# Two-layer encoder trunk: the MLP's first product in seven block products instead of eight

## The reference

```python
def sq_relu_mlp(xn, w_up, w_down):
    return jnp.square(jax.nn.relu(xn @ w_up)) @ w_down

def reference(x, ...):
    h = x
    for l in range(DEPTH):
        hn = rms_norm(h, mix_norm_g[l])
        ...
        hn = rms_norm(h, mlp_norm_g[l])
        h = h + sq_relu_mlp(hn, mlp_w_up[l], mlp_w_down[l])
    return rms_norm(h, final_norm_g)
```

## Time and profile before

| | |
|---|---|
| median of 3 runs | 2364.94 us (2364.88 to 2365.31) |
| span of the profiled execution | 2362.9 us |
| TensorE busy | 2332.4 us, 14581 matmuls |
| VectorE, ScalarE, GpSimd busy | 1462.6, 1090.2, 249.8 us |
| read from HBM | 422.79 MB, 180 GB/s |
| mean granted TensorE clock | 0.998 |
| first relu of the two MLPs | 569.04 and 1656.99 us after the span's start |

### The profile page before, as it was taken

How to read it: one execution, slowest core, us unless ns; L and a number is a source line. 1 busy time by engine, 2 the same in 40 slices (tenths; PEclk the granted TensorE clock), 3 DMA queues, 4 the chain that set the end, 5 groups by cost and what they waited for, 6 DMA issues and landing times.

```text
span 2362.9 us, 38313 instructions
## 1 busy us (share of the span) xinstructions
PE 2332.4 (99%) x14581; PEld 2108.1 (89%) x14581; DVE 1462.6 (62%) x1686; ACT 1090.2 (46%) x1391; POOL 249.8 (11%) x367
## 2 busy tenths in 40 slices
PE   8999999999999999999999999999999999999997
PEld 6888888789899999999989999998998998998996
DVE  5777777755565565565566564656555556555655
ACT  5555554435444444444445334345444444444443
POOL 4445555500000000000000000000000000000000
PEclk9999999999999999999999999999999999999999
DMA  9555555455555555555555555555555555555553
GB/s 257 162 154 157 145 152 166 145 177 170 189 192 181 192 182 194 180 193 182 190 188 176 187 180 183 192 179 178 194 180 194 181 193 182 191 183 189 189 184 125
DMA packets 316175, 425.78 MB, mean 180 GB/s; under 512 B 10537, under 2 KB 141906, under 8 KB 315986
## 3 DMA queue, kind: packets, MB, share of 16 engines
q1 hardware_dynamic: 316066, 424.92, 56.4%
q10 hardware_dynamic: 48, 0.02, 0.0%
HBM read 422.79 MB, written 2.10 MB: 180 GB/s over the span
## 4 chain that ended last, share of the span: by engine, by line
PE 87%; POOL 6%; issue 4%; ACT 1%; DVE 1%; SPq 1%; DMA 0%; POOLq 0%; DVEq 0%; ACTq 0%
PE pair L353 14%; PE pair L355 14%; PE pair L357 14%; PE m L379 11%; PE m L377 11%; PE m L375 11%; PE pair L379 3%; PE pair L375 3%; PE pair L377 3%; POOL lk L577 1%; PE m L726 1%; POOL even L564 1%; POOL kin L577 1%; PE m L790 1%; POOL lk L589 1%
## 5 line engine op out<-in xcount | busy, mean ns | idle before, releaser
L337 DVE TENSOR_TENSOR w_lo<-raw,w_hi 128x1024 fp32r<-128x1024 f32 x800 | 988.8, 1242 | 855.5 <-ACT w_hi L326 854.5
L326 ACT ACTIVATE w_hi<-raw 128x1024 fp32r<-128x1024 f32 x800 | 846.2, 1059 | 1219.3 <-PE pair L357 633.6
L379 PE MATMUL m<-xT_hi,w_lo 128*128 128x256 f32 x2176 | 615.8, 283 | 0.0
L377 PE MATMUL m<-xT_lo,w_hi 128*128 128x256 f32 x2176 | 615.8, 283 | 0.0
L375 PE MATMUL m<-xT_hi,w_hi 128*128 128x256 f32 x2176 | 615.6, 283 | 0.0
L353 PE MATMUL pair<-w_hi,yT_hi 128*128 128x512 f32 x1280 | 499.8, 391 | 1.0 <-DVE h L1208 0.9
L355 PE MATMUL pair<-w_lo,yT_hi 128*128 128x512 f32 x1280 | 498.4, 389 | 0.0
L357 PE MATMUL pair<-w_hi,yT_lo 128*128 128x512 f32 x1280 | 498.1, 389 | 0.0
L375 PEld LDWEIGHTS m<-xT_hi,w_hi 128*128 128x128 f32 x2176 | 417.7, 192 | 1.2
L377 PEld LDWEIGHTS m<-xT_lo,w_hi 128*128 128x128 f32 x2176 | 417.7, 192 | 1.2
L379 PEld LDWEIGHTS m<-xT_hi,w_lo 128*128 128x128 f32 x2176 | 417.7, 192 | 0.0
(11 more groups left out here) (147 smaller groups left out, 1711.0 us busy)
## 6 DMA issues: line engine op xcount, KB each, us to landing
raw<-in_mlp_w_up SPq DMA_DIRECT2D x128, 1024.0 KB, 5.2
raw<-in_mlp_w_down SPq DMA_DIRECT2D x128, 1024.0 KB, 5.0
raw<-in_ab_w_in SPq DMA_DIRECT2D x256, 256.0 KB, 3.9
raw<-in_conv_w_in SPq DMA_DIRECT2D x48, 1024.0 KB, 5.2
raw<-in_ab_w_out SPq DMA_DIRECT2D x64, 256.0 KB, 4.1
raw<-in_conv_w_out SPq DMA_DIRECT2D x16, 1024.0 KB, 5.0
h<-in_x SPq DMA_DIRECT2D x4, 512.0 KB, 5.9
out_dram<-h SPq DMA_DIRECT2D x8, 256.0 KB, 2.4
```

The source lines that it names most:

```text
L326: nc.scalar.activation(w_hi[:, ring], raw[:, slot, 2 * k:2 * k + 2], ACT.Copy).then_inc(hi_ready, 1)
L337: nc.vector.tensor_tensor(w_lo[:, ring], raw[:, slot, 2 * k:2 * k + 2], w_hi[:, ring].bitcast(F32), ALU.subtract).then_inc(lo_ready, 1)
L377: nc.tensor.matmul(dst[:, c], w_hi[:, ring, q, cols], xT_lo[:, kt], start=False, stop=False)
L379: mm = nc.tensor.matmul(dst[:, c], w_lo[:, ring, q, cols], xT_hi[:, kt], start=False, stop=end and c % 2 == 1)
```

## The change

The first 1024 hidden columns of an MLP stay plain, as two blocks, but with the tokens in the partitions: the normalised x is stationary (128 tokens), 512 weight columns are moving. The other 7168 columns come in seven rounds of 1024. In a round X is seen as 2x2 blocks (128 tokens by 1024 features) and the weights as 2x2 blocks B11, B12, B21, B22 of 1024 by 512, and the 2x2 result is formed by Strassen's scheme in Winograd's form: seven products P1 to P7, each of 24 matmuls of 512 columns over two slots, where plain blocks need eight.

- The sums of x (`x_sums`) are made once per MLP from an unsplit copy (`x_pair`), then split.
- Four sums of weight blocks are made in place, in two halves of 128x2048: B11+B12, then B12+B22, B11+B22 and B11+B21, the last two into the same buffer. VectorE makes five of the eight halves (`block_sum`), GpSimd issues an accumulating DMA within SBUF for three, the second halves of P7, P6 and P4.
- The order of a round is P1 D0 P5 D1 P7 D2 P6 D3 P3 D4 P4 D5 P2 D6 D7, where D0 to D7 are the slots of the second product of the round before (`down`). Some products accumulate in one PSUM bank; ScalarE copies four partial results out (`copy`), VectorE adds five times (`combine`).
- The result has tokens in the partitions, so TensorE transposes each block (`turn`, four transposes) after relu and square.
- Buffers: `raw` has 8 MB, three pairs of it for blocks and four halves for the second product's weights, which are loaded by half slots of 512 KB; the mixer's tiles now share memory with them. xT is laid out by token halves.

The diff, cut to its core:

```diff
+ROUNDS = FF // 1024
+ROUND = ["P1", "D0", "P5", "D1", "P7", "D2", "P6", "D3", "P3", "D4", "P4", "D5", "P2", "D6", "D7"]
+ROUND_AT = {name: sum(2 if u[0] == "P" else 1 for u in ROUND[:k]) for k, name in enumerate(ROUND)}
+ROUND_SLOTS = 22
+PLAIN = 8
+TAIL_AT = PLAIN + (ROUNDS - 1) * ROUND_SLOTS
+MLP_SLOTS = TAIL_AT + 8
+BLOCK_OF = {"P1": "B11", "P5": "B11", "P7": "B12", "P6": "B11", "P3": "B22", "P4": "B11", "P2": "B21"}
+SUM_OF = {"P5": ("B11", "B12"), "P7": ("B12", "B22"), "P6": ("B11", "B22"), "P4": ("B11", "B21")}
+SUMS = ["P5", "P7", "P6", "P4"]
+SUMS_DVE = [("P5", 0), ("P5", 1), ("P7", 0), ("P6", 0), ("P4", 0)]
...
+        blocks = [raw[:, 4:6], raw[:, 0:2], raw[:, 2:4]]
+        raw_d = raw[:, 6:8].rearrange("p a (b c) n -> p (a b) c n", b=2)
...
+        FORM = {"P1": (xT_hi[:, 0, 0:8], xT_lo[:, 0, 0:8]),
+                "P2": (xT_hi[:, 0, 8:16], xT_lo[:, 0, 8:16]),
+                "P4": (xT_hi[:, 1, 8:16], xT_lo[:, 1, 8:16]),
+                "P3": (xT_hi[:, 1, 0:8], xT_lo[:, 1, 0:8]),
+                "P5": (s_hi[0], s_lo[0]), "P6": (s_hi[1], s_lo[1]), "P7": (s_hi[2], s_lo[2])}
...
+                def load_block(r, block, free):
+                    if r == ROUNDS:
+                        return
+                    kt, col = 8 * (block[1] == "2"), 1024 * r + 512 * (block[2] == "2")
+                    buf = buffer_of(r, block)
+                    for k in range(2):
+                        if free is not None:
+                            sp.wait_ge(lo_ready, 2 * (free + k) + 2)
+                        sp.dma_start(blocks[buf][:, k], up[:, kt + 4 * k:kt + 4 * k + 4, col:col + 512]
+                                     ).then_inc(landed_b[buf][k], 16)
+                def load_down(r, m):
+                    cb, half = m // 2, half_of(r, m)
+                    for k in range(2):
+                        n = d_at(layer, r, m, k)
+                        if r == 1 and m < 2:
+                            sp.wait_ge(s_low, 4 * layer + (4 if (m, k) == (1, 1) else 3))
+                        else:
+                            two = (r, m - 2) if m > 1 else (r - 1, m + 6)
+                            sp.wait_ge(lo_ready, 2 * slot_of(at, two[0], f"D{two[1]}") + k + 1)
+                        kt = 8 * (r - 1) + 4 * half + 2 * k
+                        sp.dma_start(raw_d[:, n % 4], down[:, kt:kt + 2, cb * 512:(cb + 1) * 512]
+                                     ).then_inc(landed_d[n % 4], 16)
...
+                load_plain(5)
+                load_plain(6)
+                load_plain(7)
+                load_block(1, "B12", at + 4)
+                load_block(1, "B22", at + 6)
+                load_down(1, 0)
+                load_down(1, 1)
+                for r in range(1, ROUNDS):
+                    load_down(r, 2)
+                    load_down(r, 3)
+                    load_block(r, "B21", slot_of(at, r, "P7"))
+                    load_down(r, 4)
+                    load_down(r, 5)
+                    load_block(r + 1, "B11", slot_of(at, r, "P3"))
+                    load_down(r, 6)
+                    load_block(r + 1, "B12", slot_of(at, r, "P4"))
+                    load_down(r, 7)
+                    load_block(r + 1, "B22", slot_of(at, r, "P2"))
+                    load_down(r + 1, 0)
+                    load_down(r + 1, 1)
...
+            def mlp(at, layer):
+                for r in range(1, ROUNDS):
+                    for name in ("P7", "P6", "P4"):
+                        to, other = SUM_OF[name]
+                        a, b = buffer_of(r, to), buffer_of(r, other)
+                        pool.wait_ge(landed_b[b][1], block_landed(layer, r, other))
+                        if name == "P7":
+                            pool.wait_ge(sums.sem, sums.at("P51", nth(layer, r)))
+                        else:
+                            last = {"P6": "P5", "P4": "P6"}[name]
+                            pool.wait_ge(lo_ready, 2 * (slot_of(at, r, last) + 1) + 2)
+                        pool.dma_start(blocks[a][:, 1], blocks[b][:, 1], accum_op=ALU.add
+                                       ).then_inc(added[name], 16)
...
+                def product(r, name):
+                    n = nth(layer, r)
+                    if name == "P1" and r > 1:
+                        pe.wait_ge(c_made.sem, c_made.at("C22", n - 1))
+                        pe.wait_ge(copied.sem, copied.at("C21", n - 1))
+                    if name == "P7" and r > 1:
...
+                    more = name in ("P6", "P3", "P4")
+                    hi, lo = FORM[name]
+                    at_slot = slot_of(at, r, name)
+                    for k in range(4):
+                        ring = (2 * at_slot + k) % HALVES
+                        pe.wait_ge(lo_ready, 2 * at_slot + k + 1)
+                        for q in range(2):
+                            kt = 2 * k + q
+                            nc.tensor.matmul(BANK[name], hi[:, kt], w_hi[:, ring, q],
+                                             start=kt == 0 and not more, stop=False,
+                                             skip_group_check=more)
+                            nc.tensor.matmul(BANK[name], hi[:, kt], w_lo[:, ring, q],
+                                             start=False, stop=False, skip_group_check=more)
+                            mm = nc.tensor.matmul(BANK[name], lo[:, kt], w_hi[:, ring, q],
+                                                  start=False, stop=kt == 7,
+                                                  skip_group_check=more)
+                        mm.then_inc(w_used, 1)
...
+                def turn(r, c):
+                    n = made(layer, r, c)
+                    pe.wait_ge(c_sq, n)
+                    if n > 1:
+                        pe.wait_ge(c_lo, n - 1)
+                    for q in range(4):
+                        ins = nc.tensor.transpose(M[3][:, q * P:(q + 1) * P],
+                                                  c_block(c)[:, q * P:(q + 1) * P], ident[:])
+                    ins.then_inc(c_T, 1)
...
+                for r in range(1, ROUNDS):
+                    for name in ROUND:
+                        if name[0] == "P":
+                            product(r, name)
                         else:
-                            down(p - 4, at + 4 + p, 8, i, i)
-                pe.wait_ge(pair_read[0], before)
...
+                            down(r, int(name[1]))
+                        if name == "P1":
+                            turn(r - 1, "C12" if r == 1 else "C11")
+                        if name == "D0" and r == 1:
+                            turn(0, "C22")
+                        if name in ("P3", "P4", "P2"):
+                            turn(r, {"P3": "C22", "P4": "C12", "P2": "C21"}[name])
+                turn(ROUNDS - 1, "C11")
...
+                            xT_hi[:, :, kt], of_tokens(M[b], q), ACT.Copy,
                             scale=gains[:, GAIN_OF[n] + kt:GAIN_OF[n] + kt + 1])
+                        if n % 2:
+                            ins = nc.scalar.activation(
+                                x_pair(kt), of_tokens(M[b], q), ACT.Copy,
+                                scale=gains[:, GAIN_OF[n] + kt:GAIN_OF[n] + kt + 1])
                     ins.then_inc(norm_hi[n], 1)
...
+                def square(r, c):
+                    n = made(layer, r, c)
+                    if r == 0:
+                        src, scale = pair[c[2] == "2"][:, int(c[1] == "2")], 1.0
+                        if n % 4 in (3, 0):
+                            eng.wait_ge(c_T, n - 2)
+                    else:
+                        eng.wait_ge(c_made.sem, c_made.at(c, nth(layer, r)))
+                        src, scale = c_block(c), -1.0 if c in ("C12", "C22") else 1.0
+                    nc.scalar.activation(c_block(c), src, ACT.Relu, scale=scale).then_inc(c_relu, 1)
+                    eng.wait_ge(c_relu, n)
+                    nc.scalar.activation(c_block(c), c_block(c), ACT.Square).then_inc(c_sq, 1)
...
+                for r in range(1, ROUNDS):
+                    for name in ROUND:
+                        slot = slot_of(at, r, name)
+                        if name == "D0":
+                            hidden_hi(r - 1, "C12" if r == 1 else "C11")
+                        if name == "P5" and r == 1:
+                            hidden_hi(0, "C22")
+                        if name in ("D4", "D5", "D6"):
+                            hidden_hi(r, {"D4": "C22", "D5": "C12", "D6": "C21"}[name])
+                        if name == "D4":
+                            copy(r, "C21")
+                        split(slot + 2)
+                        if name[0] == "P":
+                            split(slot + 3)
+                        if name in ("P1", "P5", "P6"):
+                            copy(r, {"P1": "P1", "P5": "C22", "P6": "C12"}[name])
+                        if name in ("D3", "D4", "D5", "D6"):
```

(54 more changed lines are left out.)

503 lines of the change are left out of this document (321 added, 182 removed).

## The result

The changed kernel takes 2352.06 us (median of 4 runs, 2350.45 to 2354.02) where the kernel before takes 2364.93 on the same chip: ratio 0.9945, 95% interval 0.9931 to 0.996. It is 12.9 us faster. The forecast was 61 us faster, and 2352 lies above 2348, the top of its range. The profiled execution has a span of 2350.0 us, 2.1 less than the median.

A forecast was written before the change was run, and what follows sets the result against it. The prediction took TensorE's instruction stream to bound the two MLPs: 2364.9 less 91.4 of TensorE work, plus 21 of lateness in the rounds and 9 at the MLP starts, gave 2303.5, stated as 2304, range 2275 to 2348 us.

The forecast's parts named there:

- Where it is late: Walk of three engines through a round and each MLP start: TensorE late 1.5 us a round (21 us), 9 at the starts.
- the paragraph on SP's queue: Second-product weight loads: D7's the tightest, landed near 69, wanted at 71, covered by 2 us; if not, 14 us.
- Spacings 0.120 and 0.2267 us: Start-to-start distances of 256- and 512-column matmuls on TensorE; the wider form saves 20.4 us per layer.
- Transposes 0.1 each: New TensorE transposes of the hidden block: 128 a layer at 0.1 us each, 12.8 us.
- VectorE 72.3 us a round: VectorE's splits, block sums, combinations and hidden low parts in a round, against 83.2 us of TensorE: 87% busy.
- A round of 84.8: Length of a round expected in the changed profile, about 84.8 us; TensorE's own work in it 83.2.
- P5 late by 0.4: In each round P5's first low part ends at 11.7 us, TensorE wants it at 11.3: late 0.4.
- P6 late by 1.1: In each round P6's low part comes at 34.4 us, wanted at 33.5: late 0.6, and 0.5 in its next entries.
- The accumulating DMA at 10 us: Each of three a round taken as twice a plain load, 10 us; P7's has 12 us free, so no cost.
- The third rival: Kernel slower because P7's accumulating DMA is the bound: at 20 us, 9.2 late a round and 2432 us; chance 12%.
- Second rival: VectorE binds in the product slots: 87.4 us a round, 4.2 above TensorE's 83.2, kernel at 2341 us; chance 16%.
- The norm block's extra activations: Eight more ScalarE activations a layer: 8.0 us in two slots, swallowed by four entries of lead; otherwise 3.6 a layer.

The follow-up runs named there:

- e1: Changed kernel with the unsplit copies of x in memory free at that time, so D0's loads wait less: 2341.54 us, ratio 0.99.
- e2: Changed kernel with only the hidden blocks' high and low parts moved earlier in ScalarE's and VectorE's queues at each MLP start: 2315.61 us, ratio 0.9793.
- w_wide: Kernel before, first product with x stationary and 512 weight columns moving, needed transposition left out: 2323.67 us, 41.3 us less, ratio 0.9828.
- v0: e4 without VectorE's five half sums and the waits for them, so part of the computation is missing: 2290.86 us, ratio 0.9687.
- d0: e4 without the three accumulating DMAs a round and ScalarE's waits for them, so three half sums are missing: 2306.18 us, ratio 0.975.
- g1: e4 with the high and low part of the fourth sum of x made later: 2301.76 us, ratio 0.9735, the fastest full version.
- f1: e4 with the second half of P5's block sum made after P5's first low parts: 2344.55 us, ratio 0.9913.
- e4: Changed kernel with the edits of e1 and e3 together, the fourth low part in D1's step: 2306.28 us, ratio 0.975.
- e3: Changed kernel with e2's edits, three sums of x split one slot earlier and the fourth high part after the squares: 2308.23 us, ratio 0.9758.

## Why the prediction was wrong

**The step that failed** is one sentence of "Where it is late": at the start of each MLP "4.5 us a layer, 9 in both". The stops are 20.9 and 20.5 us, and the lower clock behind them costs about 12 more. (The two terms of that sentence, 3.0 and 1.1, add to 4.1 and not 4.5; it changes nothing here.) Three things were left out:

1. I walked VectorE's work at the start only up to D0 and P5, and never asked what D0's buffer was used for until then. The diff has the answer in one line, `sp.wait_ge(s_low, ...)`: the load of D0 waits for VectorE. In the paragraph on SP's queue only D7 was walked, the tightest load of a running round; the first of the first round was the late one. e1 prices it at 10.5 us.
2. `turn` waits for a low part that stands in VectorE's order behind two splits or two sums. I counted it as 2.4 us of work in the round, and not as a wait of TensorE with work queued in front. e2 prices it at 36.4 us with its share of the clock, the high part on ScalarE included.
3. A stop has a second price. The earlier trace rows showed a clock of 1.00, and I carried it over without a word on what happens once TensorE stops; the half-speed stretches cost about 7.5 us in the first MLP and 4.2 in the second.

**What held**, each by its own term:

- Spacings 0.120 and 0.2267 us: w_wide gives 41.3 for 40.8.
- Transposes 0.1 each: 0.11, and 0.2 us more a round. TensorE's round of 83.2 was 84.1 in v0, most of the rest in the matmuls on `tail`.
- VectorE 72.3 us a round: 72.8; the block sum of 2.2 to 2.4: 2.285 busy.
- A round of 84.8: 85.04, 4 us over 14 rounds, from two errors that nearly cancel: TensorE's own round 0.9 too low, the lateness 1.5 forecast and 0.9 there.
- P5 late by 0.4: 0.34 idle, each round, 0.5 by the starts. P6 late by 1.1: hardly (0.16).
- The accumulating DMA at 10 us, free below 12: it lands in 8.6 (median; 6.9 to 9.7), and d0 shows that it costs nothing. The third rival falls. The estimate from the two pages of the Trainium skill (DMA: Bandwidth & Descriptors, "Measured (HBM→SBUF, 128 partitions, SWDGE, issued from GpSimd)"; Collectives: The Full Stack, "The bandwidth ceiling") was 12.3 us and about 1 us of start; the measurement is well under that.
- Second rival, VectorE as the bound of a round: no at five half sums, and at eight the round is 87.5, close to the 87.4 that the rival gave for five, by chance.
- The norm block's extra activations: no stop shows in their slots.
- The convolution's matmuls with the moving operand in two runs, costed at nothing: they start 0.120 us apart in the changed kernel too (1399.81 to 1401.73 us, 16 distances).

With the starts mended the sum of the prediction stands: 2304 forecast, 2301.8 measured in g1. That the forecast and the mended kernel meet within 3 us is in part luck: it rests on the two errors in the round that cancel. What stays open: why matmuls on `tail` stand further apart, and whether the 0.9 us of VectorE's lateness can go; f1 tried the one way and lost.

## What to carry to other kernels

Walk the first pass of a loop as carefully as the steady round: its buffers come from somebody else, its order is pasted from what stood there, and its waits have no round before them to hide in. When a queue is written out by hand, put an item where its waiter needs it, not where its data is ready: here a subtraction of 0.68 us behind two sums and four splits held the bounding engine for 4 us, and the clock after it. For each new wait of the bounding engine, ask what stands queued in front of the instruction that ends it, and for each new load, who has to be finished with its buffer.

## What was not expected of the hardware

- An accumulating DMA within SBUF, 128x2048 float32 added in place, takes GpSimd 0.87 us to issue and lands in 6.9 to 9.7 us beside engines that are 77% busy; taking three a round away changes nothing (d0 against e4: 0.1 us).
- Matmuls of the same shape stand 0.2333 us apart with the stationary operand in `tail`, 0.227 with it in `xT` or `yT`. That the place is the cause is not shown.
- The price of a TensorE stop is not given by its length. Behind the stops of e4 (0.34 to 1.05 us idle) stands no stretch of matmuls 0.43 apart. In e3 a stop of 1.67 us and one of 0.50 right after it have six such matmuls behind them in the first MLP, and the same two stops have none in the second. Behind the 2.1 us stop of f1 there was such a stretch in seven rounds of twelve. Of the stops of 3 to 7 us in the changed kernel seven had one. The eighth, the first stop of the second MLP, as long as that of the first MLP, had none:

```profile
1670.38 0.63 PE L1106 MATMUL m<-ident,blk 128*128 128x128 f32 x4 [3.16 <-DVE yT_lo L1800]
...
1671.09 0.39 PE L434 MATMUL pair<-w_lo,xT_hi 128*128 128x512 f32 x1
1671.31 0.40 PE L436 MATMUL pair<-w_hi,xT_lo 128*128 128x512 f32 x1
```
